# Five of the 2 MB expert-weight loads issued as one 112-row and two 8-row transfers

## The reference

```python
logits = ht @ router_w + router_b
top_vals, top_idx = lax.top_k(logits, TOP_K)          # 4 of 32
combine = ...                                          # softmax weights, 0 for experts not chosen
for e in range(N_EXPERTS):                             # 32
    gu = ht @ w_gate_up[e] + b_gate_up[e]              # 1024 x 2048
    gate, up = gu[:, :D_FF], gu[:, D_FF:]
    act = min(gate, 7) * sigmoid(1.702 * gate) * (clip(up, -7, 7) + 1.0)
    out = out + combine[:, e:e + 1] * (act @ w_down[e] + b_down[e])   # 1024 x 1024
```

## Time and profile before

| | |
|---|---|
| median of 3 runs | 1237.72 us (1237.39 to 1237.72) |
| profiled execution, its own time | 1237.29 us |
| its span, first to last instruction | 1235.4 us |
| TensorE (PE) busy | 1160.8 us, 94% of the span |
| VectorE (DVE), ScalarE (ACT) busy | 420.2 us, 266.9 us |
| moved by DMA | 455.25 MB, mean 368 GB/s |
| wide loads | 116 of `w_gate_up`, 54 of `w_down`, 2048 KB each |

### The profile page before, as it was taken

How to read it: one execution, slowest core, us unless ns; L and a number is a source line. 1 busy time by engine, 2 the same in 40 slices (tenths; PEclk the granted TensorE clock), 3 DMA queues, 4 the chain that set the end, 5 groups by cost and what they waited for, 6 DMA issues and landing times.

```text
span 1235.4 us, 13704 instructions
## 1 busy us (share of the span) xinstructions
PE 1160.8 (94%) x5828; PEld 599.6 (49%) x5828; DVE 420.2 (34%) x703; ACT 266.9 (22%) x422; POOL 0.2 (0%) x4
## 2 busy tenths in 40 slices
PE   7999999999999999999999889888988898889987
PEld 6899968888533443443343324333433333333332
DVE  6777878756421221222112112111221121111112
ACT  6866546344210000010010001000100010000002
POOL 0000000000000000000000000000000000000000
PEclk9999999999999999999999999999999999999999
DMA  9454425698999999999999999999999999999996
GB/s 322 147 157 151 148 91 171 217 399 340 365 425 428 427 428 428 427 429 425 429 426 429 428 428 428 427 428 428 427 428 425 429 427 429 427 429 427 427 426 263
DMA packets 67292, 455.25 MB, mean 368 GB/s; under 512 B 6970, under 2 KB 23771, under 8 KB 39966
## 3 DMA queue, kind: packets, MB, share of 16 engines
q1 hardware_dynamic: 65654, 454.06, 89.8%
q10 hardware_dynamic: 1576, 0.29, 0.1%
HBM read 453.29 MB, written 1.05 MB: 368 GB/s over the span
## 4 chain that ended last, share of the span: by engine, by line
PE 64%; DMA 32%; DVE 2%; issue 1%; ACT 1%; DVEq 0%; ACTq 0%
DMA ring<-in_w_gate_up 28%; PE bank L1201 18%; PE bank L1219 12%; PE total L902 6%; PE bank L902 5%; PE total L890 4%; PE bank L890 4%; DMA ring<-in_w_down 3%; PE bank L960 2%; PE bank L1187 2%; PE bank L979 1%; PE total L1233 1%; PE total L1201 1%; PE bank L1208 1%; PE total L950 1%
## 5 line engine op out<-in xcount | busy, mean ns | idle before, releaser
L1201 PE MATMUL bank<-ring,hy_area 128*64 128x512 f32 x1984 | 444.6, 595 | 43.2 <-DMA ring<-in_w_gate_up 43.2
L1201 PEld LDWEIGHTS bank<-ring,hy_area 128*64 128x64 f32 x1984 | 136.8, 137 | 331.4 <-issue 244.6
L1219 PE MATMUL bank<-ring,xn_area 128*64 128x512 f32 x992 | 220.1, 595 | 0.3 <-DMA ring<-in_w_down 0.3
L2119 DVE TENSOR_SCALAR qk_area<-bank 128x512 f32<-128x512 f32 x31 | 21.4, 692 | 361.3 <-PE bank L1201 361.3
L1219 PEld LDWEIGHTS bank<-ring,xn_area 128*64 128x64 f32 x992 | 68.4, 137 | 134.6 <-issue 122.8
L1682 ACT ACTIVATE qk_area<-qk_area 128x512 f32<-128x512 f32 x32 | 20.2, 630 | 456.7 <-DVE qk_area L2119 456.7
L2130 DVE SCALAR_TENSOR_TENSOR xn_area_r<-bank,tmp_area,xn_area_r 128x512 fp32r<-128x512 f32 x31 | 23.3, 751 | 200.5 <-ACT xn_area_r L1693 200.5
L1823 DVE TENSOR_TENSOR front_r<-ring,slot_r 128x1024 fp32r<-128x1024 f32 x60 | 73.1, 1222 | 22.2 <-ACT slot_r L1493 22.2
L1493 ACT CAST slot_r<-ring 128x1024 fp32r<-128x1024 f32 x60 | 62.8, 1049 | 43.5 <-PE bank L902 23.2
L1693 ACT ACTIVATE xn_area_r<-bank,tmp_area 128x512 fp32r<-128x512 f32 x31 | 21.3, 687 | 234.9 <-PE bank L1219 221.0
L979 PE MATMUL bank<-tmp_area_r 128*128 128x512 f32 x124 | 38.0, 426 | 12.8 <-issue 8.6
(11 more groups left out here) (397 smaller groups left out, 1253.2 us busy)
## 6 DMA issues: line engine op xcount, KB each, us to landing
ring<-in_w_gate_up SPq DMA_DIRECT2D x116, 2048.0 KB, 37.0
ring<-in_w_down SPq DMA_DIRECT2D x54, 2048.0 KB, 38.9
ring<-in_w_in SPq DMA_DIRECT2D x31, 1024.0 KB, 5.7
ring<-in_w_gate_up SPq DMA_DIRECT2D x22, 1024.0 KB, 9.4
ring<-in_w_down SPq DMA_DIRECT2D x19, 1024.0 KB, 9.9
ring<-in_w_branch_gla SPq DMA_DIRECT2D x4, 1024.0 KB, 5.2
ring<-in_w_branch_hy SPq DMA_DIRECT2D x4, 1024.0 KB, 7.7
ring<-in_w_out SPq DMA_DIRECT2D x4, 1024.0 KB, 6.3
```

Source lines behind the costliest of these rows:

```text
L1201: last = pe.matmul(to[bk][half * CAP:(half + 1) * CAP, :], xeT[:, j, q, :], where(j, c), start=False, stop=(j == GU_CH - 1), skip_group_ch ...
L1219: last = pe.matmul(banks[to][half * CAP:(half + 1) * CAP, :], half_of(turned, f), where(j, c * D + half * 512), start=(f == 0), stop=(f == ...
L2119: nc.vector.tensor_scalar(gate, made[0][:, :], LIMIT, None, ALU.min).then_inc(gate_ready, 1)
```

## The change

A new function `row_parts(n)` names the row ranges into which the load of chunk `n` is cut. For five of the 170 wide loads (list positions 8, 42, 76, 110 and 144 among the wide ones; chunk numbers 52, 120, 188, 256 and 324) it gives rows 0 to 111, 112 to 119 and 120 to 127; for all others the whole 128 rows. `moe` issues one transfer per range, and `expert_arrivals` counts 16 increments for each. Four of the five loads are of `w_gate_up`, one (188) of `w_down`. The bytes, their places and the order of all loads are the same.

```diff
+EVEN_ROWS = 112
+FEW_ROWS = 8
+SPLIT = tuple(n for n, width in LOADS if width == 2)[8::34]
+
+
+def row_parts(n):
+
+    if n not in SPLIT:
+        return [(0, P)]
+    return [(0, EVEN_ROWS)] + [(r, r + FEW_ROWS) for r in range(EVEN_ROWS, P, FEW_ROWS)]
+
+
 def expert_arrivals():
 
     count, arrival = [0] * SLOTS, {}
@@ -198,7 +211,7 @@
         if n in ASIDE:
             continue
         s = slot_of(n)
-        count[s] += 16
+        count[s] += 16 * len(row_parts(n))
         arrival.update({n + i: (s, count[s]) for i in range(width)})
     return arrival
 
@@ -766,7 +779,9 @@
             def moe(n, width=1):
 
                 s = slot_of(n)
-                sp.dma_start(ring[:, s * SLOT:(s + width) * SLOT], rows_of(*CHUNK_ORDER[n], width)).then_inc(moe_loaded[s], 16)
+                src = rows_of(*CHUNK_ORDER[n], width)
+                for r, to in row_parts(n):
+                    sp.dma_start(ring[r:to, s * SLOT:(s + width) * SLOT], src[r:to, :]).then_inc(moe_loaded[s], 16)
```

## The result

The changed kernel takes 1294.87 us (median of 4 runs, 1289.85 to 1299.40) against 1237.61 us before: 57 us more, ratio 1.0461 with a 95% interval of 1.0446 to 1.0477. The profiled execution took 1296.85 us, its span is 1295.1 us, 59.7 us over the span of before. The direction was forecast, the size was not: 1258 us and a range up to 1277 us.

The account below looks back on a forecast made before the run. The never-pausing weight stream was taken to bound the kernel. Small parts cost 24.4 us over five loads, less 3.5 us slack, the 112-row part 0: 21 us on 1237.3, so 1258 us, range 1235 to 1277.

Parts of the forecast that it names:

- What bounds the kernel: From 400 to 1200 us the weight stream never pauses; whatever lengthens it moves the end by as much.
- Issues and semaphores at nothing: Ten more SyncE transfers, 3.3 us in all, hidden by the queue; higher semaphore counts add no wait: cost nothing.
- The 112-row part: Rows 0 to 111 of each split load: between 0 and half rate, 21 us in all; taken as 0.
- The lead of the engines: Engines finishing early at the stream's end, read as slack: 3.5 us taken off the cost once.
- Price of an 8-row transfer: Each small part of a split load takes between 0.61 and 4.9 us; the middle, 2.75 us, was taken.
- The sum: Five split loads at 4.9 us more on the small parts' engines, 24.4 us, less 3.5 slack: 21 us.
- Balance, in part or in full: Early engines take the rows: held by one engine, 1236.9 us (0.16 with no effect); in full, 1234.2 us (0.19).
- the wrong half: Rows cost 0.61 us but go to the late engines: +3.06 us, 1240.4 us; chance 0.05.
- Crowding at its full size: 8-row transfers at 4.9 us, 1280 us, or 112-row part at its bound, 1279 us; within crowding's 0.60.
- The range: Whole run between 1235 and 1277 us, said to reach up to where both bounds would meet.
- The signs: If crowding: five dips below 420 GB/s about 167 us apart, waits of several us, longer end slope, TensorE busy 1160 us.

Follow-up runs that it names:

- experiment 4: Against the kernel before: the five loads come as two transfers of all 128 rows, half the columns each; 1238.07 us, +0.2 us.
- experiments 5: Against the kernel before: five neighbouring wide loads (wide positions 8 to 12) come as 64 + 64 rows; 1264.23 us, +26.6 us.
- experiment 6: Against the kernel before: only the last of the five loads comes as 64 + 64 rows; 1248.84 us, +11.2 us.
- experiment 3: Against the kernel before: the five far-apart loads come as two transfers of 64 rows; 1283.78 us, +46 us.

## Why the prediction was wrong

*What bounds the kernel.* Right. Time lost in the stream at 405 us, when TensorE is 99% busy, reached the end as fully as time lost late: 26.6 us for five cuts there and 26.1 us by the windows, 11.2 us for one cut at 1070 us and 11.2 us by the windows.

*Issues and semaphores at nothing.* Right as far as tried, +0.2 us for five more transfers in experiment 4.

*The 112-row part: this step failed.* Its bounds were 0 and 21 us (half rate), and 0 was taken because 112 is near 128. It measured 20.4 us. The nearest row in count was the wrong guide: loads cut to 112, 64 or 32 rows all ran at 214 to 241 GB/s, all 128 at 428. For these counts the halving that the earlier trace rows showed was the whole effect at once, and not the first step of a scale. Why 112 rows halve the rate stays open. A reading that fits is that the rate depends on how rows are dealt to the engines, and that with any deal but that of a 128-row load they get in each other's way. But no trace here shows which engine carried a row, and no run tells whether the loss is where the rows are read or where they are written.

*The lead of the engines: this term was missing.* The sum priced the cut load alone. By theory A2, which forecast experiments 5 and 6, a cut load halves the rate of its neighbours in the queue too, as long as some engines are in it and others are not. The lead was in the prediction, read from the earlier trace rows as 3 to 6 us, and it was entered with the wrong sign: as slack that would take 3.5 us off once. It was paid in full at each of the five loads, 25 us more than if they had been neighbours. That it grows along the stream, from about 2 to 6 us, is why the later dips are longer. In the changed kernel the last dip loses more still, 14.0 us where it is 10.8 us with 64 rows and 11.5 us with 112 and 16. The 18 us slope at the end fits that its uneven parts had pulled single engines further apart.

*Price of an 8-row transfer.* Over-sized: 1.5 us (0.9 to 2.1 by the intervals) where 2.75 was taken. The 2.4 us that the prediction estimates from the Trainium skill, "SBUF — State Buffer", section "Door 1: The DMA port swizzle", was nearer but too long as well. The ten of them make 15 us, not 27.5. The reason for the difference wasn't tried; it may be that engines reach such a transfer up to G apart and need not all crowd at once.

*The sum.* 24.4 - 3.5 + 0 = 21 was forecast; 15.1 - 3.1 for the small parts (12 us over their plain price), 20.4 for the 112-row part and 24.9 for the lead were measured, 57 us. The small parts were priced at twice what they cost (24.4 against 12), the 112-row part was taken at the wrong one of its two bounds, and the lead came in as a gain. The first error hid a part of the other two; without that luck the forecast would have been further off, at about 1246 us.

*The rivals.* Balance, in part or in full, and the wrong half assumed that a row costs 0.61 us wherever it goes; the dips put all three out. Crowding at its full size was nearest. Its 1279 us had the 112-row part at its bound, its 1280 us had the 8-row transfers at theirs; neither had both, and both lacked the lead.

*The range.* The prediction says that its upper end, 1277 us, is where both bounds would meet. It isn't: by its own numbers that is 46 + 21 - 3.5 us, 1301 us, and even its full crowding, at 1279 and 1280 us, lay outside. The measured 1294.87 us is under 1301, though not for the reason given: the 46 us of small parts would have stood in for the lead.

*The signs.* Five dips under 420 GB/s came, 173 to 177 us apart (167 and what the dip between adds), and so did waits of several us and a longer slope. TensorE's busy time didn't stay at 1160.8 us, it is 1178.6 us: see below.

## What to carry to other kernels

In a stream like this one, at 427 to 429 GB/s with a full queue, a load cut by rows (112, 64 or 32 of 128) does not cost by its own size: the rate is about half for as long as any engine is in it, so it loses its own time plus the lead of the first engine over the last. Read that lead from how the engines drop out at the end of the stream, and add it to each such load, or put such loads next to each other (26.6 us in place of 46). Where the bounds of a term are 0 and a full halving, and the trace shows a halving for anything like it, take the halving.

## What the runs showed of the hardware

A cut by columns, two pieces of 8 KB a row, is free (+0.2 us for five), a cut by rows is not: 112 and 16, two times 64, and four times 32 rows cost 45, 46 and 44 us for the same five loads.

SyncE needed 0.67 us for each 8-row transfer with rows four apart (10.74 / 16), and 0.34 us with neighbouring rows (5.40 / 16).

The engines of a stream that is never idle drift apart: some 2 us between the first and the last at 405 us (experiment 3), some 6 at 1070 us (experiment 6) and at the end. What holds the last ones back wasn't tried.

TensorE's granted clock fell after long waits. With only the last load cut, the stretch behind its dip reads (windows of 5 us):

```profile
1075.00:1080.00 5.00, 5.00 (x24) 1.97 (x23) 1.33 (x3) 0.58 (x1) 0.00 (x0) 1.00 0.98 210
1080.00:1085.00 5.00, 0.08 (x2) 0.00 (x0) 0.00 (x0) 0.00 (x0) 0.00 (x0) 0.85 0.98 174
1085.00:1090.00 5.00, 4.55 (x12) 1.47 (x14) 0.00 (x0) 0.00 (x0) 0.00 (x0) 0.50 1.02 223
```

TensorE was all but idle from 1080 to 1085 us, and in the next 5 us it had 0.50 of its clock, the 1.2 GHz level: 12 matmuls in 4.55 us of busy time, where 24 had taken 5.00. In the changed kernel the matmuls on gate and up take 611 ns in the mean, not 595, and 459.3 us of busy time, not 444.6: most of the 18 us more. By the sum above (59 of 59.7 us found in the stream) the slower clock cost next to nothing, since TensorE waits for the stream anyway.
